# A streaming encoder layer on one core: the front end run in two waves of 256 and 384 tokens, with 168 row gathers in the second

## What is computed

```
p  = x @ w_in                       # 2048 x 8448: A q,k,v | B q,k,v | gate A | gate B
yA = chunk attention, 16 heads, own chunk of 64 + 8 before, relative-position bias
yB = sliding-window attention, 16 query heads on 2 key heads, ALiBi, sinks
m  = sigmoid(gA) * (yA @ w_proj_a) + sigmoid(gB) * (yB @ w_proj_b)
h  = LayerNorm(alpha * x + m @ w_out)
q  = h @ w_query                    # 8 heads, two halves of 128 each
v1,i1 = top16(q1 @ keys1.T); v2,i2 = top16(q2 @ keys2.T)
sc,e  = top16 of the 256 sums v1+v2 # 16 of 128*128 experts for each head and token
w  = softmax(sc) * gelu(u_table[e] . h)
y  = LayerNorm(alpha * h + sum over the 128 picks of w * v_table[e])
```

## Time and profile before

| | us |
|---|---|
| median of 3 runs | 4467.98 (4462.01 to 4469.11) |
| span of the profiled execution | 4456.8 |
| PE busy | 4282.4 |
| DVE busy | 2839.1 |
| POOL busy | 2672.1 |
| ACT busy | 1376.0 |

### The profile page before, as it was taken

One profiled execution on the slowest core, in us unless ns is written; L12 is line 12 of the kernel. 1 busy time (PEld: TensorE's weight loads), 2 busy tenths in 40 slices (PEclk: granted clock), 3 DMA queues, 4 the chain that ended last, 5 costly groups with the idle time before them and its releaser, 6 DMA issues.

```text
span 4456.8 us, 71381 instructions
## 1 busy us (share of the span) xinstructions
PE 4282.4 (96%) x26508; PEld 4120.7 (92%) x26508; DVE 2839.1 (64%) x4233; ACT 1376.0 (31%) x2750; POOL 2672.1 (60%) x1665
## 2 busy tenths in 40 slices
PE   8999999999989999799899999999999999999998
PEld 8999888878879999699899999999999999999997
DVE  1000133444442231699997899898997988988988
ACT  1000122222221110311386434343443443443444
POOL 5444322222324545244776778778887888888884
PEclk9999999999999999999999999999999999999999
DMA  5222233222233323112489999999999999999995
GB/s 202 99 102 98 96 119 128 104 81 81 78 119 122 116 90 99 38 66 76 145 276 320 382 376 398 374 372 409 416 405 377 412 418 411 417 411 416 418 418 241
DMA packets 269138, 1083.82 MB, mean 243 GB/s; under 512 B 24560, under 2 KB 90224, under 8 KB 185328
## 3 DMA queue, kind: packets, MB, share of 16 engines
q0 software_dynamic: 74736, 544.24, 29.8%
q1 hardware_dynamic: 89568, 391.16, 23.6%
q10 hardware_dynamic: 104736, 147.39, 9.7%
HBM read 1020.44 MB, written 67.63 MB: 244 GB/s over the span
## 4 chain that ended last, share of the span: by engine, by line
PE 66%; DVE 18%; DMA 6%; issue 5%; POOL 3%; ACT 1%; ACTq 0%; DVEq 0%; POOLq 0%
PE banks L497 30%; PE banks L741 15%; PE banks L675 11%; DVE work L1499 3%; DVE work L1462 2%; DVE banks L1465 2%; POOL w_lo L383 2%; PE banks L729 2%; DMA work<-in_u_rows,idx_all 2%; PE banks L566 2%; PE banks L528 2%; DMA work<-in_v_rows,idx_all 1%; POOL work L411 1%; PE banks L536 1%; DVE work L1371 1%
## 5 line engine op out<-in xcount | busy, mean ns | idle before, releaser
L383 POOL TENSOR_TENSOR w_lo<-w_raw,w_hi 128x1024 fp32r<-128x1024 f32 x472 | 1140.7, 2417 | 243.5 <-ACT w_hi L1057 229.6
L389 POOL TENSOR_SCALAR w_hi<-w_raw 128x2048 fp32r<-128x2048 f32 x134 | 289.6, 2161 | 1326.8 <-PE banks L497 1252.3
L497 PE MATMUL banks<-mv_hi,w_hi 128*128 128x256 f32 x3648 | 863.2, 318 | 62.9 <-DVE mv_lo L1203 35.4
L497 PE MATMUL banks<-mv_lo,w_hi 128*128 128x256 f32 x3648 | 835.8, 310 | 0.0
L497 PE MATMUL banks<-mv_hi,w_lo 128*128 128x256 f32 x3648 | 835.3, 310 | 0.0
L497 PEld LDWEIGHTS banks<-mv_hi,w_hi 128*128 128x128 f32 x3648 | 652.1, 189 | 127.1 <-issue 85.9
L741 PE MATMUL banks<-mv_hi,w_hi 128*128 128x384 f32 x2048 | 693.2, 338 | 43.5 <-ACT part_t L1116 22.1
L393 POOL TENSOR_TENSOR w_lo<-w_raw,w_hi 128x512 fp32r<-128x512 f32 x536 | 721.0, 1377 | 11.2
L675 PE MATMUL banks<-mv_hi,w_hi 128*128 128x384 f32 x2048 | 694.0, 339 | 4.6 <-ACTq L1083 2.0
L741 PE MATMUL banks<-mv_lo,w_hi 128*128 128x384 f32 x2048 | 690.3, 337 | 0.0
L741 PE MATMUL banks<-mv_hi,w_lo 128*128 128x384 f32 x2048 | 690.3, 337 | 0.0
(11 more groups left out here) (166 smaller groups left out, 5319.5 us busy)
## 6 DMA issues: line engine op xcount, KB each, us to landing
w_raw<-in_wstream SPq DMA_DIRECT2D x472, 512.0 KB, 7.9
w_raw<-in_wstream SPq DMA_DIRECT2D x134, 1024.0 KB, 4.8
gate_matrix<-work ACTq DMA_DIRECT2D x12, 2048.0 KB, 9.0
work<-gate_matrix ACTq DMA_DIRECT2D x32, 768.0 KB, 9.0
out_p<-work ACTq DMA_DIRECT2D x34, 320.0 KB, 2.2
work<-out_p ACTq DMA_DIRECT2D x34, 320.0 KB, 3.4
gate_scratch<-work ACTq DMA_DIRECT2D x32, 320.0 KB, 2.2
work<-gate_scratch ACTq DMA_DIRECT2D x16, 640.0 KB, 4.0
```

Source lines behind the costliest of these rows:

```text
L383: pool.tensor_tensor(w_lo[s][:, part], raw[s][:, part], w_hi[s][:, part].bitcast(f32), ALU.subtract) \
L389: pool.tensor_scalar(w_hi[s][:, :], raw[s][:, :], 1.0, 0.0, ALU.mult, ALU.add).then_inc(hi_done, 1)
L497: last = pe.matmul(acc(dst, h), a[s][:, P * k:P * k + P], b[h][:, k, :], start=(k == k_first and n == 0), stop=(k == k_last and n == 2))
```

## The change

**Two waves.** The front end runs twice over its 114 weight units. The first wave takes the 256 tokens whose experts are gathered (columns 0 to 255), the second the other 384. `k_step` has three matmuls for a row block instead of six. The 114 MB of weights are loaded and split twice, and each wave has its own attention, projections, LayerNorm, queries and picks.

**Splitting.** ACT makes the high half of every unit, POOL only the low one, as the late part did before; that holds for the whole kernel now, also for the 20 PEER units ahead of the late part.

**Gathers.** After the first wave's picks (`top_picks(0, i)`, two blocks), `FRONT` = 168 of the 512 gathers run in the second wave, from its 14th unit on, into four buffers of their own (`rows_front`). `deal_front` spreads them: about 2.35 for each of the 21 remaining q, k, v units, 1.5 for a gate unit, 2 for a projection unit, 2.5 for a w_out unit. 12 stay in the gate-matrix stage, and `deal` spreads the other 332 over the late part.

**Attention.** A step is one block of 128 queries with both heads of the pair. The scores of the two heads are issued one behind the other in pieces of 256 columns, into two banks; so are the products with the values, into the two halves of one bank. One bank `t_bank` serves all transposes and value products in turn: each use (`turn`) waits until ACT has taken the use before it (`take`). ACT loads the operands of the next pair one pair ahead. In the second wave the gate units have one accumulator bank, not two.

The core of the diff:

```
-WAVES = ((0, N1), (N1, N2))
+COLS = (0, 2 * P)
+NW = (2 * P, T - 2 * P)
+BLOCKS = ((0, "sample"), (1, 2, 3))
+FRONT = 168
...
-                for n, (a, b) in enumerate(((w_hi, mv_hi), (w_hi, mv_lo), (w_lo, mv_hi))):
-                    for h in range(2):
-                        last = pe.matmul(acc(dst, h), a[s][:, P * k:P * k + P], b[h][:, k, :],
+                for z, (a, b) in enumerate(((w_hi, mv_hi), (w_hi, mv_lo), (w_lo, mv_hi))):
+                    last = pe.matmul(dst, a[s][:, P * k:P * k + P], b[w][:, k, :],
...
+                    for lo in range(0, wide, 2 * P):
+                        hi = min(lo + 2 * P, wide)
+                        for hh in range(2):
+                            rows = slice(HD * hh, HD * hh + HD)
+                            last = pe.matmul(s_bank[w][hh][:, lo:hi], q_t[w][par][rows, q_end - P:q_end],
+                                             k_t[w][par][rows, end - wide + lo:end - wide + hi], start=True, stop=True)
...
+            def turn(w, use):
+                kind, at, hh, (lo, hi) = use
+                if T_ORDER[w][use]:
+                    pe.wait_ge(t_taken, T_AT[w] + T_ORDER[w][use])
...
+                    for j in range(len(parts)):
+                        if uses:
+                            take(w, uses[j])
+                        if j == len(parts) - 1 and sg < STEP_TOTAL[w]:
+                            for hh in range(2):
+                                exponents(w, sg, hh)
+                        for g, k in parts[j]:
+                            if k == KT_N // 2 - 1:
+                                first_half_read(WAVE[w] + U_GATE + g)
+                            if k == KT_N - 1:
+                                gate_evacuate(w, g)
+                                weights(WAVE[w] + U_GATE + g + 2, 1)
...
+            natural(1)
+            qkv_pair(1, 0)
+            pe.wait_ge(hb_taken, 1)
+            natural(0)
+            with pe.Fori(1, N_QKV // 2) as i:
+                qkv_pair(1, i)
+            attention(1)
```

More of the change, by code:

```diff
@@ L68, with deal_front @@
 STEPS = deal()
-STEPS_LAST = max(k for k, s in enumerate(STEPS) if s)
+SLOT_0 = 13
+def deal_front():
+    share = [0] * U_FRONT
+    for m in range(SLOT_0, N_QKV):
+        share[m] = 7 / 3
+    for m in range(U_GATE, U_PROJ):
+        share[m] = 1.5
+    for m in range(U_PROJ, U_OUT):
+        share[m] = 2
+    for m in range(U_OUT, U_QUERY - 1):
+        share[m] = 2.5
+    scale = FRONT / sum(share)
+    steps, total, n = [], 0, 0
+    for m in range(U_FRONT):
+        total += share[m] * scale
+        upto = min(FRONT, round(total))
+        steps.append(list(range(n, upto)))
+        n = upto
+    steps[U_QUERY - 2] += list(range(n, FRONT))
+    return steps
@@ L72, in place @@
+FRONT_STEPS = deal_front()
 def place(n):
-    return n % (ROWS - 1) if n < FIRST else n % ROWS
+    if n < FRONT:
+        return n % ROWS
+    return ROWS + ((n - FRONT) % (ROWS - 1) if n < GATE_END else n % ROWS)
+PLACES = [place(n) for n in range(STEP_END + ROWS)]
 def arrivals(n):
[L79 to L96, removed]
+    return sum(PLACES[m] == PLACES[n] and m != STEP_NORM + 3 for m in range(n + 1))
+def step_before(n):
+    return next((m for m in range(n - 1, -1, -1) if PLACES[m] == PLACES[n]), None)
+STEP_TOTAL = [len(BLOCKS[w]) * 2 * PAIRS for w in range(2)]
@@ L192, in build @@
[L192 to L203, removed]
@@ L647, in _ @@
-            pe.wait_ge(lsum_done, 1 + N_OUT)
-            layer_norm(0)
-            def key_scores(s, c):
-                pe.wait_ge(q_evac, c + 3)
-                pe.wait_ge(sc_taken, c + 1)
-                four, one = sc_parts(s)
-                for b in range(NB):
-                    out = four[:, P * b:P * b + P] if b < 4 else one
-                    last = pe.matmul(out, qe[s][:, P * b:P * b + P], subkt[:, KEYS * s:KEYS * s + KEYS],
-                                     start=True, stop=True)
-                last.then_inc(sc_full, 1)
@@ new lines, in key_scores, with query @@
+            def key_scores(w, c):
+                pe.wait_ge(q_evac, Q_AT[w] + c + 3)
+                pe.wait_ge(sc_taken, Q_AT[w] + c + 1)
+                for b in range(NB[w]):
+                    last = pe.matmul(banks[:, 2 + c % 2, P * b:P * b + P], qe[w][c % 2][:, P * b:P * b + P],
+                                     subkt[:, KEYS * (c % 2):KEYS * (c % 2) + KEYS], start=True, stop=True)
+                last.then_inc(sc_full, 1)
+            def query(w):
+                for c in range(N_QUERY):
+                    pe.wait_ge(q_evac, Q_AT[w] + c + 1)
+                    unit(w, WAVE[w] + U_QUERY + c, c % 2, acc(w, c % 2), "h", (lambda: key_scores(w, c - 1)) if c else None)
+                key_scores(w, N_QUERY - 1)
@@ L837, in _, with weights, first_half_read @@
-            act.sem_inc(qkv_evac, 2)
-            load_moving(x_t, 0, (), first=True)
+            for w in range(2):
+                act.sem_inc(g_stored[w], 16)
+            def weights(n, h):
+                s, part = n % 2, HALVES[h]
+                act.wait_ge(raw_half[s][h], 16 * (n // 2) + 16)
+                act.activation(w_hi[s][:, part], raw[s][:, part], ACT.Copy).then_inc(hi_done, 1)
+            def first_half_read(n):
+                act.wait_ge(half_read, halves_read(n) + 1)
+                weights(n + 2, 0)
```

1636 lines of the change are left out of this document (875 added, 761 removed).

## The result

The changed kernel takes 4507.8 us (median of 4 runs, 4503.4 to 4508.1), the kernel before 4465.9 in runs taken with it: ratio 1.0082, 95% interval 1.0065 to 1.0098. It is slower by 42 us, where I had forecast 27 faster. The range, 4365 to 4540, holds it. The profiled executions are 4506.3 and 4456.8 us long.

A forecast was written before the change was run, and what follows sets the result against it. PE was taken to set the time nearly everywhere. Terms -27 - 50 + 24 + 44 - 48 + 30 = -27 us took 4456.8 to 4430, or 4441 us as median; own range 4400 to 4480, whole 4365 to 4540.

The forecast's parts named there:

- Matmuls of the weights, 0: Front end's weight matmuls: two waves take the same 14.09 us a unit, no gain, if the weight load hides under 120 ns.
- Small matmuls, -27 and -50: Attention: -27 us from entries paid once for two heads, less waiting; -50 from the two heads partly overlapping.
- the bound of -90: Attention: far end of the gain from overlapping heads, half the stream time; the other end is 0, the middle -50.
- the heads don't overlap: Rival, attention: the same sum without the 50 us of overlap, +23, 4491 us; chance 0.24.
- ACT's queue, +24: First wave's attention: ACT's queue takes 4.5 us against PE's 2.4; 1.5 us a pair over 16, +24 us.
- ACT's queue binds in both waves: Rival, attention: each of 80 steps loses 0.9 us more than counted, price 72 us, +45, 4513 us; chance 0.22.
- Seams, +44: Stage boundaries, now two of each: attention +18, drain +6, projections +16, w_out +5, ahead of late part +5, start -6.
- LayerNorm scales with the columns and is paid in two parts: Between w_out and late part: LayerNorm's cost splits by columns over the waves; that whole stretch 602 us against 596.5, +5.
- Picks by blocks, 25.6 us a head for three: Ahead of the late part: 41.03 us a head for five blocks scaled to about 25.6 for the second wave's three.
- The start, -6: Kernel start: 2 MB of x are loaded, not 5, -6 us.
- Second wave's DMA, +30: Second wave's q, k, v, w_out and projections beside gathers: at 418 GB/s 12, 15 and 3 us longer, +30.
- Late part, -48: Late part: loses a third of its gathers and recovers all but 18 of its 66 lost us, -48.

The follow-up runs named there:

- the order mended: Changed kernel with ACT issuing attention's next-pair loads behind the copies out of the transpose bank, not all at the step's start: 4444.8 us, ratio 0.9942 to the kernel before.
- all seven edits: Changed kernel with loads behind copies, early bank release, POOL low-part quarters, 144 gathers, tables spread, first pair early, x splits ahead of picks: 4364.1 us, ratio 0.9768.
- the run with quarters: Changed kernel with POOL making each half of a unit's low part in two instructions of 512 columns, not one of 1024: 4489.4 us, ratio 1.0047.
- its run: Changed kernel with 144 gathers in the second wave, not 168; the 24 taken from w_out units go to the late part: 4491.1 us, ratio 1.0043.

## Why the prediction was wrong, point by point

The sign failed in two places: the work moved onto ACT's queue in the first attention, priced at +24 without the clock behind its waits, and the stretch ahead of the late part, where +67 us came for +5 and four steps failed. Attention takes 822 us, above the 807 that the prediction named as a sign of being wrong.

**Matmuls of the weights, 0: right.** 1536 matmuls of 256 columns in the first wave take 186.6 us in the chain, 121.5 ns each with the slow start in them; the load hides under them.

**Small matmuls, -27 and -50: right in kind, too small.** I took the middle between no overlap and half the stream time. The overlap is whole: 0.70 and 0.70, 1.12 and 1.13. Attention without waits, gate units and what the time at 1.2 GHz cost (half of it, an estimate) went from some 339 to some 225 us, so about -114 where the two terms hold some -117 with the bound of -90. The sentence that failed is that starts stay in the program's order, so that only one head's second instruction can run with the other's first: the heads' first instructions start 6 ns apart. The Trainium skill (TensorE: Matmul & The Clock Gate, part 3) says that distinct row groups run concurrently, and the rows agree; it also says that starts stay in program order, and these rows don't bear that out. The rival *the heads don't overlap* falls with it. The term of -27 was added up wrongly besides: its parts, -1.7, +0.5 and -1.2, are -2.4 a pair, -38 in all.

**ACT's queue, +24: the right place, the wrong price.** The queue, the copy behind it and its 4.5 us against 2.4 were as I wrote. I gave 1.5 us a pair; the wait is 2.05 on average, 2.7 where it is shown, and behind it come 3.0 us of the lower clock, which I had not thought of. With the order mended 63 us come back. This is the mechanism of the rival *ACT's queue binds in both waves*, and its 4513 is near the result, yet it binds in the first wave alone (second wave: 23 waits ahead of the transposes, 16 us). In attention as a whole waits and clock cost some 118 us more than before, where queue, starts and drain were priced at 48; the small matmuls give back 37 more than forecast.

**Seams, +44: the larger part of the miss.** Four steps failed:
- "LayerNorm scales with the columns and is paid in two parts": it left out a release. Before, the first query unit began beside the scaling; now it waits 15.1 and 20.1 us for the end of it. The diff showed it, two lines moved. 18 us.
- Picks by blocks, 25.6 us a head for three: 27.1 measured, some 12 us over eight heads. For two blocks the same scaling gives 16; it is 19 to 21 in heads without a split of x and 27 to 31 with two. Some steps of DVE last until POOL's split ends (as the conversion above does), and the change made these longer, 2.42 us for 1024 columns against 1.38 for 512. I took the earlier trace rows for work of DVE alone, though POOL split beside it then too, and for a typical head, where it is the longest of seven (37.2 to 41.0). PE waits 23.0 us for the last picks (L818) against 9.6 before, and still 20.0 with all seven edits, so that no run gave this part back:

```profile
PE banks L711 <- DVE work L1438: 9.6, 1, 9.6
```

- The splits of x stand behind the picks on DVE, and PE waited 9.2 us; 11 us by the run with quarters. I had named every queue but this one.
- The residual's last sum behind gathers, 14.8 us: I had costed the gathers in DMA time only, not as DVE steps that stand ahead of a sum. 17 us by its run.

The starts of attention were 13.9 and 23.9 us, 38 and not 24 together, the second with the gathers' transfers in its way.

**The start, -6: wrong, and by one more queue.** 20 us of table issues stand on ACT's queue ahead of the third unit's high part. 11 us.

**Second wave's DMA, +30: wrong place.** Nothing in q, k, v at 421 GB/s; some 46 us at the start of attention, in it and in w_out, part of it DVE's steps.

**Late part, -48: right**, -52 with the end.

## What to carry to other kernels

When work moves to another engine, walk through that engine's queue from start to end and ask what each moved instruction now stands ahead of: here the same loads and table issues that cost nothing before cost 74 us once weights and bank copies shared their queue, and an order mended in a few lines gave it back. A short wait of PE with small matmuls behind it has to be priced with the clock that follows, which here doubled it. And the time of an engine that was stretched by another does not scale with its columns: look at who ran beside it when its rows were taken.

## What was new about the hardware

- Two heads on disjoint halves of the array cost what one costs: 0.70 us for one or two against 256 keys, 1.09 for values over four blocks of one head (kernel before) or of both. In the trace their instructions start 6 ns apart, out of program order. With eight of one head ahead of the other's, values over four blocks take 1.58, with six over three blocks 1.15 and not 0.88; with four there is no loss.
- The granted clock fell to 1.2 GHz behind each of 14 waits of 1.2 to 3.4 us with 16 small matmuls after them, in the case shown for 6.8 us of unbroken work; behind waits of 1.0 to 2.5 us with a transpose and weight matmuls after them it stayed at 2.4.
- One small instruction of DVE lasted 6.21 us, through three of POOL's in a row: shorter instructions on POOL don't bound the stretch if they follow each other (6.59 us beside six of half the length).
- One transfer of a table's constant part kept ACT's queue for 7.07 us at its issue, where the loads of a pair take 0.42 to 0.84.
